# Reordering three edges of a long one-core kernel and parting the attention's queries and keys

## The chip, the cores and the metric

The kernel runs on one core of a Trainium2 chip. Time is device microseconds (us) from a run of the whole program, and a comparison uses the median of several runs. The engines are PE (TensorE), DVE (VectorE), ACT (ScalarE), POOL (GpSimd) and SP (SyncE, used here to issue transfers); each works through its own list of instructions in order, and they meet through semaphores.

## The reference

Two blocks follow each other for one sequence of 512 tokens and 1024 features, in fp32. The first has two layers: an RWKV-7 time mix with its MLP, then forgetting attention with its MLP. The second has an mLSTM branch, which also reads 256 context tokens, and a Fourier branch. Cut to the three things that the change touches:

```
# RWKV-7 time mix: the decay, and the output with its bonus
w_log = -softplus(-(w0 + tanh(xw @ w1) @ w2)) - 0.5
decay = exp(-exp(w_log))
y     = group_norm(wkv7_scan(r, decay, k, v, -kk, kk * a)) * ln_w + ln_b
bonus = sum_over_head(r * k * r_k) * v
out   = ((y + bonus) * g) @ wo
# forgetting attention: 16 heads of 64, F = cumsum(log_sigmoid(f_logit))
q, k  = rms_norm(q, q_gain), rms_norm(k, k_gain)
s     = q @ k.T / sqrt(64) + F[t] - F[s],   s <= t
o     = softmax(s) @ v
x     = x + (1 + gt1) * ((o * sigmoid(gate)) @ w_o)
# mLSTM branch: modulated inputs of the latents and of the context
h     = rmsnorm(x, g) * (1 + sc) + sh
hc    = rmsnorm(ctx, g) * (1 + scc) + shc
```

## The kernel before

Everything lies feature-major: a tile is 128 features by 512 tokens, so a matrix of 1024 features by 512 tokens is eight tiles. The context's tiles are 128 by 256. Weights are streamed as blocks of 128 x 2048 words, 1 MB each, in two buffers of `wraw`. SP issues a block's load once the block two before it has been split (`load_weights`, line 480). POOL splits each block into a high part `whi` that fp32r holds exactly (line 530) and the remainder `wlo` (line 534), in `split_weights`. PE then multiplies in three fp32r products, `whi`·high, `whi`·low and `wlo`·high (`block_of`, line 586; `block_by_tile`, line 618). The inputs of each product are parted in the same way: ACT rounds to the high part, DVE subtracts for the low part. In the names below `...h` and `...l` (`oh`, `ol`, `hh`, `hl`, `h2h`, `h2l`) are these parts.

The order of the work is written out by hand: each engine has a function per phase, and what an engine does next is what stands next in its text. Four places matter.

**Decay reads** (RWKV inputs, ACT). `high(n)` does n pieces of one input's mix, each a `keep` (line 1157) and a `round_mix` (line 1164). `hidden` reads a hidden tile of the gate from PSUM (line 1176) and rounds it (line 1181). Then eight reads of the decay products into `cum` (line 1176 as well, in `read_out`) free the PSUM banks that PE writes them into.

**Bonus additions** (end of the RWKV layer, POOL). In this stretch POOL first splits two weight blocks, that of `g2` and the first of `wo`, then adds the bonus to the normed output in eight tiles (line 1638). DVE gates each sum (line 1533), ACT rounds it (line 1504), DVE takes the low part (line 1538), and PE multiplies by `wo`. SP's queue holds in this order: a modulation block, two loads of weights (line 480), another modulation block (line 1457), the modulation row (line 1463, needed by ACT's Silu, line 1508), and six more blocks. DVE's line 1525 multiplies these blocks with the row; its results scale the residual additions (line 1550).

**Attention.** The eight pairs of heads have four query tiles each: 32 steps s, with s // 4 the pair i and s % 4 the query tile t. A step has two items n (its two heads). PE runs, for each step, `scores` (two 64-row products of `q_sb` with `kk_sb`, line 2590, then for each head the forget sums, line 2594, and the mask, line 2596), `turn` (transposes of the exponentials, line 2606) and, per pair, `values` (line 2616) and `spread_sums` (line 2625). DVE takes the maximum (line 2768); ACT takes the exponential (line 2693) and copies the turned ones (line 2702). PE issues the scores of a step ahead of the turns of the step before. DVE also normalises the next pair's queries and keys (`norm`, line 2760; gains from line 2576) and gates, weighs and parts the output (lines 2782, 2787, 2791), of which ACT rounds the high part (line 2708). The products of `scores` are fp32 products:

```
pe.matmul(ps[:, score_bank(2 * s + h), :w], q_sb[rr, i, P * t:P * t + P],
          kk_sb[rr, i, :w], start=True, stop=False)
```

**Start of the mLSTM.** DVE works out the latents' norm in a chain of small operations (lines 693, 3207, 3209), copies a column of it (line 3210), then scales and parts the first two context tiles (`h_run(0, 2)`: lines 3189 and 3195), with ACT's rounding between them (line 3120). PE's first product there (line 2988) waits for the low part `h2l`. ACT's root for the second norm (line 3123) stands in front of those roundings.

Of the kernel before, what the change touches and what calls it, by code (L numbers as in the profile page):

```python
# [16 lines left out]
F32 = mybir.dt.float32  # L17
# [364 lines left out]
def program(nc, A, out, plan, vat, cat):  # L382
    ctx = ExitStack()
    with ctx:
# [553 lines left out]
        with nc.Block() as block:  # L938
# [207 lines left out]
            def _(act):  # L1146
# [75 lines left out]
                hidden_half(1, ACT.Copy)  # L1222
                act.wait_ge(*hid_ready.at(2))
                for n in range(2):
                    high(3)
                    hidden(hidg[:, n], ACT.Sigmoid, sgh[:, n])
                high(2)

# [4 lines left out]
                for g in range(KT):  # L1233
                    read_out(cum[:, g], ACT.Sigmoid, V("w0", g))
                    if g == 3:
                        qk_read_out(act, 0, 7)
                    elif g == 6:
                        fold_read_out(act, 0, 7)
# [193 lines left out]
        with nc.Block() as block:  # L1432
# [183 lines left out]
            @block.gpsimd  # L1616
            def _(pool):
                def stepped(o):
                    o.then_inc(*inverse_step.inc())
                    pool.wait_ge(*inverse_step.at(inverse_step.made))  # L1620
                for hf in HALVES:
                    pool.wait_ge(*blk_in.at(16 * (hf + 1)))
                    for s in range(1, 31):
                        n = 31 - s
                        part = tmp[:, :s * n].rearrange("p (i j) -> p i j", j=n)
                        row = tt[:, s:s + 1, s + 1:].broadcast_to([P, s, n])
                        col = tt[:, 0:s, s:s + 1].broadcast_to([P, s, n])
                        stepped(pool.tensor_tensor(part, row, col, ALU.mult))
                        stepped(pool.tensor_tensor(tt[:, 0:s, s + 1:], tt[:, 0:s, s + 1:], part, ALU.add))
                    stepped(pool.memset(tt.rearrange("p s t -> p (s t)")[:, 0::33], 1.0))  # L1630
                    pool.tensor_copy(tn, tt.rearrange("p s t -> p t s")).then_inc(*inverted.inc())
                pool.wait_ge(*corrected_by.at(nth["ER", 3, 1][1]))
                pool.memset(yrows[:].bitcast(F32), 0.0).then_inc(*y_cleared.inc())
                split_weights(pool, firsts["wo"][1] + 1)
                for p in range(KT):
                    pool.wait_ge(*vb_shifted.at(p + 1))
                    pool.wait_ge(*by_dve.at(nth["SP", p][1]))
                    pool.tensor_tensor(r_sb[:, p], r_sb[:, p], arena[:, 25 + p], ALU.add).then_inc(*y_added.inc())
                project_pool(pool)
# [870 lines left out]
        pr, ptr = tiles("pr", 64, 4), [tiles(f"ptr{b}", 8 + 4 * b, 4) for b in range(4)]  # L2510
        oh, ol = tiles("oh", 48, KT, F32R), tiles("ol", 32, KT, F32R)
        sums = fixed("sums", [P, 4, 2, 4])
        top = fixed("top", [P, 4])
        NI, NS = 8 * KT, 4 * KT
        phase_start()
        with nc.Block() as block:
# [6 lines left out]
            rooted, inverted, root_high = signal("qk_rooted"), signal("qk_inverted"), signal("root_high")  # L2523
            gain_spread, pair_normed = signal("scale_spread"), signal("qk_normed")
            scored, topped, raised = signal("scores"), signal("max_ready"), signal("exp_done")
            turned, copied, totalled = signal("p_turned"), signal("p_copied"), signal("values_done")
# [8 lines left out]
            def score_bank(n):  # L2535
                return n % 4
# [16 lines left out]
            def _(pe):  # L2553
# [25 lines left out]
                def scores(s):  # L2579
                    i, t = s // 4, s % 4  # L2580
                    if t == 0:
                        pe.wait_ge(*pair_normed.at(2 * i + 2))
                    if s >= 2:
# [3 lines left out]
                    w = P * (t + 1)  # L2587
                    for h in range(2):
                        rr = slice(64 * h, 64 * h + 64)
                        pe.matmul(ps[:, score_bank(2 * s + h), :w], q_sb[rr, i, P * t:P * t + P], kk_sb[rr, i, :w], start=True,  # L2590
                                  stop=False)
                    for h in range(2):
# [73 lines left out]
            def _(act):  # L2666
# [29 lines left out]
                def copy(n):  # L2696
# [3 lines left out]
                    if t == 0 and i >= 2:  # L2700
# [3 lines left out]
                                   ACT.Copy).then_inc(*copied.inc())  # L2704

                def round_of(i):
                    act.wait_ge(*weighted.at(i + 1))
                    act.activation(oh[:, i], otile[:], ACT.Copy).then_inc(*rounded.inc())
# [21 lines left out]
                for k in range(KT):  # L2730
                    read_g(k)
                fold_read_out(act, 11, 4)
                exp(0)
                exp(1)
                for n in range(NI):
# [3 lines left out]
                    if n % 8 == 3 and n > 8:  # L2739
                        round_of(n // 8 - 1)  # L2740
                round_of(KT - 1)
                squares_of_x(act, x_squared, x_added, 5)
# [3 lines left out]
            def _(dve):  # L2746
# [10 lines left out]
                def norm(i, j):  # L2757
                    x, gain = ((q_sb, qgs[:, 0:1]), (kk_sb, V("kg", 0)))[j]
                    dve.wait_ge(*gain_spread.at(2 * i + j + 1))
                    dve.scalar_tensor_tensor(x[:, i], x[:, i], gain, ps[:, VALUES if j else SPREAD], ALU.mult,  # L2760
                                             ALU.mult).then_inc(*pair_normed.inc())

                def maximum(n):
# [41 lines left out]
                norm(0, 0)  # L2805
                norm(0, 1)
                maximum(0)
                maximum(1)
                for s in range(NS):
                    i, t = s // 4, s % 4  # L2810
                    if t == 0 and i:
                        sum_inverse_of(i - 1)
                    if t == 2 and i + 1 < KT:
                        norm(i + 1, 1)
                    if s + 1 < NS:
# [5 lines left out]
                    elif t == 1 and i + 1 < KT:  # L2821
                        norm(i + 1, 0)
                    if t == 2 and i:
                        part(i - 1)
# [53 lines left out]
        with nc.Block() as block:  # L2878
# [194 lines left out]
            def _(act):  # L3073
# [43 lines left out]
                def round_h(n):  # L3117
                    src, gain, norm, shift, k, part, width = h_of(n)
                    act.wait_ge(*scaled.at(n + 1))
                    act.activation(h2h[:, k, part], ps[:, 4 + n % 2, :width], ACT.Identity, bias=shift).then_inc(*rounded.inc())  # L3120
                root(act, rooted)
                act.wait_ge(*mean_made.at(2))
                act.activation(stat2[:, 1], ps[:, 7, 8:12], ACT.Sqrt, bias=C("epsn")).then_inc(*rooted2.inc())
                fold_read_out(act, 14, 2)
                for n in range(KT + 3):
                    round_h(n)
# [57 lines left out]
            def _(dve):  # L3184
# [13 lines left out]
                def h_run(lo, hi):  # L3198
# [4 lines left out]
                    part_h(hi - 1)  # L3203
                dve.memset(gacc[:], 0.0).then_inc(*VE.up(sem("dve")))
                inverse_root(dve, rooted, inverted)
# [3 lines left out]
                dve.tensor_tensor(ps[:, 7, 8:12], ps[:, 7, 8:12], stat[:, 1], ALU.mult).then_inc(*mean_made.inc())  # L3209
                dve.tensor_copy(stat2[:, 0], stat[:, 1]).then_inc(*VE.up(sem("dve")))  # L3210
                h_run(0, 2)
                dve.wait_ge(*rooted2.at(1))
                dve.reciprocal(ps[:, 7, 12:16], stat2[:, 1]).then_inc(*gain_made.inc())
                dve.wait_ge(*gain_made.at(1))
                dve.tensor_tensor(stat2[:, 2], ps[:, 7, 12:16], stat[:, 1], ALU.mult).then_inc(*inverted2.inc())
                h_run(2, KT)
                dve.wait_ge(*spread2.at(1))
                h_run(KT, 2 * KT)
                chain = sem("dve")
                dve.wait_ge(*VE.last())  # L3220
# [910 lines left out]
```

## Time and profile before

| | us |
|---|---|
| median of 3 runs | 2545.86 (2544.88 to 2550.26) |
| profiled execution | 2549.13 |
| its span, with a mean granted TensorE clock of 0.987 | 2547.3 |
| attention, first scores to last values | 1027.8 to 1131.9 of the span |

The profiled execution is 3.3 us above the median of the runs. The times in the rows further down count from the start of its span. In a timeline row come start, length, engine, line, operation, what is written and what is read, tile shapes, and the number of neighbouring instructions that the row joins; lengths of neighbouring instructions can overlap, since a pipeline takes the next before the last has ended. In brackets stands the idle time before and what ended it. PEld is PE loading weights; SPq and ACTq are issues of transfers.

### The profile page before, as it was taken

What the parts mean: (1) busy time and instruction counts of PE and PEld (TensorE: products, weight loads), DVE (VectorE), ACT (ScalarE), POOL (GpSimd) and SP (SyncE); (2) the same over time, 40 slices, a digit from 0 to 9 for tenths busy, and PEclk for the clock granted to TensorE, in tenths of its full rate; (3) what the DMA queues carried; (4) which work ended last, traced back from release to release, by engine and by line L of the source; (5) the groups of instructions that cost most, each with busy time, mean ns of one, the idle gap of its engine ahead of it and who ended that gap; (6) DMA issues with size and microseconds to landing.
All of it is one profiled execution on the core that took longest, in us unless ns stands there. A gap on an engine that the chain in (4) does not pass through costs nothing. (4 is left out here: it accounts for less than half of the span.)

```text
span 2547.3 us, 36273 instructions
## 1 busy us (share of the span) xinstructions
PE 2452.7 (96%) x14664; PEld 1925.6 (76%) x14664; DVE 1245.2 (49%) x1849; ACT 743.6 (29%) x1439; POOL 1536.1 (60%) x784
## 2 busy tenths in 40 slices
PE   5999988999999999999999999999999999999998
PEld 4777766788888777667888877888775478787886
DVE  7647257775562244454444437877485643121112
ACT  5744423331120212543311212333324431111210
POOL 6874717677777776016988873533262067754774
PEclk9999999999999999999999999999999999999999
DMA  7322436566652222104656522323334273311221
GB/s 276 108 83 80 121 97 264 211 243 231 231 215 93 99 90 99 40 18 142 228 206 229 214 100 95 117 116 116 151 138 147 102 303 126 114 66 67 83 99 66
DMA packets 90334, 358.28 MB, mean 141 GB/s; under 512 B 27337, under 2 KB 41289, under 8 KB 52946
## 3 DMA queue, kind: packets, MB, share of 16 engines
q1 hardware_dynamic: 65712, 229.79, 24.9%
q10 hardware_dynamic: 24482, 126.50, 13.1%
q8 instruction: 103, 1.69, 0.3%
q14 instruction: 37, 0.30, 0.0%
HBM read 317.18 MB, written 39.06 MB: 140 GB/s over the span
## 5 line engine op out<-in xcount | busy, mean ns | idle before, releaser
L530 POOL TENSOR_TENSOR whi<-wraw,con_sb 128x512 fp32r<-128x512 f32 (+1 forms) x305 | 622.0, 2059 | 826.8 <-PE ps L586 606.5
L534 POOL TENSOR_TENSOR wlo<-wraw,whi 128x512 fp32r<-128x512 f32 (+1 forms) x305 | 796.4, 2632 | 12.9
L586 PE MATMUL ps<-hh,whi 128*128 128x512 f32 x936 | 365.7, 391 | 0.0
L586 PE MATMUL ps<-hh,wlo 128*128 128x512 f32 x936 | 364.2, 389 | 0.0
L586 PE MATMUL ps<-hl,whi 128*128 128x512 f32 x936 | 364.2, 389 | 0.0
L586 PEld LDWEIGHTS ps<-hh,whi 128*128 128x128 f32 x936 | 175.7, 188 | 41.0 <-issue 4.3
L586 PEld LDWEIGHTS ps<-hh,wlo 128*128 128x128 f32 x936 | 175.7, 188 | 36.7
L586 PEld LDWEIGHTS ps<-hl,whi 128*128 128x128 f32 x936 | 175.7, 188 | 35.9
L586 PE MATMUL ps<-midh,whi 128*128 128x512 f32 x512 | 199.7, 390 | 0.0
L586 PE MATMUL ps<-midh,wlo 128*128 128x512 f32 x512 | 199.2, 389 | 0.0
L586 PE MATMUL ps<-midl,whi 128*128 128x512 f32 x512 | 199.2, 389 | 0.0
L2373 DVE TENSOR_TENSOR midl<-rsq,midh 128x512 fp32r<-128x512 f32 x64 | 110.6, 1729 | 153.8 <-ACT midh L2330 153.8
L586 PE MATMUL ps<-h2h,whi 128*128 128x512 f32 (+1 forms) x464 | 173.6, 374 | 0.8 <-ACT hb L3635 0.7
L586 PE MATMUL ps<-h2l,whi 128*128 128x512 f32 (+1 forms) x464 | 171.3, 369 | 0.0
L586 PE MATMUL ps<-h2h,wlo 128*128 128x512 f32 (+1 forms) x464 | 171.1, 369 | 0.0
L2216 DVE SCALAR_TENSOR_TENSOR cond_w<-cond_w,ps 128x1024 f32<-128x1024 f32 x136 | 159.9, 1211 | 0.0
L2324 ACT ACTIVATE relu<-ps 128x512 f32<-128x512 f32 x64 | 38.3, 599 | 381.4 <-PE ps L586 364.9
L2379 DVE SCALAR_TENSOR_TENSOR x<-ps,mod,x 128x512 f32<-128x512 f32 x64 | 48.0, 750 | 189.1 <-PE ps L586 189.1
L586 PEld LDWEIGHTS ps<-midh,whi 128*128 128x128 f32 x512 | 96.1, 188 | 20.9 <-issue 1.1
L586 PEld LDWEIGHTS ps<-midh,wlo 128*128 128x128 f32 x512 | 96.1, 188 | 20.1
L586 PEld LDWEIGHTS ps<-midl,whi 128*128 128x128 f32 x512 | 96.1, 188 | 19.7
L3240 DVE SCALAR_TENSOR_TENSOR ps<-xm,vec_sb,ps 128x441 f32<-128x441 f32 (+3 forms) x160 | 105.1, 657 | 5.2
(518 smaller groups left out, 4618.5 us busy)
## 6 DMA issues: line engine op xcount, KB each, us to landing
wraw<-wst SPq DMA_DIRECT2D x162, 1024.0 KB, 4.8
cond_w<-wcond ACTq DMA_DIRECT2D x68, 1024.0 KB, 4.8
first_w<-wcond SPq DMA_DIRECT2D x8, 1024.0 KB, 14.0
mod_w<-wcond SPq DMA_DIRECT2D x8, 1024.0 KB, 13.4
d_v<-key_and_query ACTq DMA_DIRECT2D x4, 1536.0 KB, 5.4
d_s<-ssb ACTq DMA_DIRECT2D x4, 1536.0 KB, 5.2
sld<-d_s SPq DMA_DIRECT2D x4, 1536.0 KB, 6.3
vld<-d_v SPq DMA_DIRECT2D x16, 384.0 KB, 3.5
```

What stands on the lines that cost most here:

```text
L530: o = pool.tensor_tensor(whi[:, s, c], wraw[:, f, c], C("zero").broadcast_to([P, width]), ALU.add)
L534: o = pool.tensor_tensor(wlo[:, s, c], wraw[:, f, c], whi[:, s, c].bitcast(F32), ALU.subtract)
L586: o = e.matmul(ps[:, b, :nt], w[:, k, mc], x[:, k0 + k, t0:t0 + nt], start=first and k == 0 and j == 0, stop=final and k == nk - 1 and j == 2)
L2216: o = dve.scalar_tensor_tensor(cond_w[n % 2][:, m], cond_w[n % 2][:, m], 1.0, row_at[r], ALU.mult, ALU.mult, accum_out=cond_to[layer][2 * ...
L2324: act.activation(relu[:, n % 4], ps[:, b], ACT.Relu).then_inc(*AC.up(acc_free[b]))
L2373: dve.tensor_tensor(midl[n // KT % 2][:, n % KT], rsq[:, n % 4], midh[n // KT % 2][:, n % KT].bitcast(F32), ALU.subtract).then_inc(*mid_lo ...
L2379: dve.scalar_tensor_tensor(x_sb[:, m], ps[:, b], mod[layer][:, 40 + m:41 + m], x_sb[:, m], ALU.mult, ALU.add).then_inc(*VE.up(acc_free[b]))
L3240: dve.scalar_tensor_tensor(dst, src, w(kh, kw), dst, ALU.mult, ALU.add).then_inc(*VE.up(chain))
```

## The change

**Decay reads.** The two `hidden` reads follow each other, and the three pieces that stood before the second and the two behind it move: one behind the pair, one each behind reads 0, 1, 3 and 5 of `cum`. The first three stay.

**Bonus additions.** The split of `wo`'s first block moves behind the first four additions.

**Attention.** Queries and keys of a pair are parted: ACT rounds each into the new tile `qk_high` (two pairs deep), DVE subtracts to get the low parts, which lie in `oh` (queries) and `ol` (keys) until the output is written there. `scores` makes six fp32r products of 64 rows per step, high·high, high·low and low·high for each of the two heads. For pair i+1 ACT rounds in the loop behind items 3 and 4 of pair i, and DVE subtracts in pair i's step t = 2, behind the maxima. The first scores of a pair wait for `qk_parted` instead of `qk_normed`. The key's `norm` moves from t = 2 to t = 1, `part` of the output from t = 2 to t = 3.

**Start of the mLSTM.** DVE scales two context tiles ahead of the norm's chain and parts them behind the mean, ACT rounds them ahead of the second root. The copy goes (a reciprocal in its place behind the context's tiles), and the clearing of `gacc` moves behind all tiles.

```diff
@@ -1223,6 +1223,6 @@
                 act.wait_ge(*hid_ready.at(2))
+                high(3)
                 for n in range(2):
-                    high(3)
                     hidden(hidg[:, n], ACT.Sigmoid, sgh[:, n])
-                high(2)
+                high(1)
 
@@ -1234,2 +1234,4 @@
                     read_out(cum[:, g], ACT.Sigmoid, V("w0", g))
+                    if g in (0, 1, 3, 5):
+                        high(1)
                     if g == 3:
@@ -1633,4 +1635,5 @@
                 pool.memset(yrows[:].bitcast(F32), 0.0).then_inc(*y_cleared.inc())
-                split_weights(pool, firsts["wo"][1] + 1)
                 for p in range(KT):
+                    if p % 4 == 0:
+                        split_weights(pool, firsts["wo"][1] + p // 4)
                     pool.wait_ge(*vb_shifted.at(p + 1))
@@ -2511,2 +2514,3 @@
         oh, ol = tiles("oh", 48, KT, F32R), tiles("ol", 32, KT, F32R)
+        qk_high = tiles("qk_high", 70, 4, F32R)
         sums = fixed("sums", [P, 4, 2, 4])
@@ -2524,2 +2528,3 @@
             gain_spread, pair_normed = signal("scale_spread"), signal("qk_normed")
+            qk_rounded, qk_parted = signal("qk_rounded"), signal("qk_parted")
             scored, topped, raised = signal("scores"), signal("max_ready"), signal("exp_done")
@@ -2581,3 +2586,3 @@
                     if t == 0:
-                        pe.wait_ge(*pair_normed.at(2 * i + 2))
+                        pe.wait_ge(*qk_parted.at(2 * i + 2))
                     if s >= 2:
@@ -2587,6 +2592,7 @@
                     w = P * (t + 1)
-                    for h in range(2):
-                        rr = slice(64 * h, 64 * h + 64)
-                        pe.matmul(ps[:, score_bank(2 * s + h), :w], q_sb[rr, i, P * t:P * t + P], kk_sb[rr, i, :w], start=True,
-                                  stop=False)
+                    high, at = qk_high[:, 2 * (i % 2):2 * (i % 2) + 2], slice(P * t, P * t + P)
+                    for n, (q, k) in enumerate(((high[:, 0], high[:, 1]), (high[:, 0], ol[:, i]), (oh[:, i], high[:, 1]))):
+                        for h in range(2):
+                            rr = slice(64 * h, 64 * h + 64)
+                            pe.matmul(ps[:, score_bank(2 * s + h), :w], q[rr, at], k[rr, :w], start=n == 0, stop=False)
                     for h in range(2):
@@ -2705,2 +2711,8 @@
 
+                def round_qk(i, j):
+                    act.wait_ge(*pair_normed.at(2 * i + j + 1))
+                    if i >= 2:
+                        act.wait_ge(*scored.at(8 * i - 8))
+                    act.activation(qk_high[:, 2 * (i % 2) + j], (q_sb, kk_sb)[j][:, i], ACT.Copy).then_inc(*qk_rounded.inc())
+
                 def round_of(i):
@@ -2731,2 +2743,5 @@
                     read_g(k)
+                    if k == 5:
+                        round_qk(0, 0)
+                        round_qk(0, 1)
                 fold_read_out(act, 11, 4)
@@ -2740,2 +2755,4 @@
                         round_of(n // 8 - 1)
+                    if n % 8 in (3, 4) and n // 8 + 1 < KT:
+                        round_qk(n // 8 + 1, n % 8 - 3)
                 round_of(KT - 1)
@@ -2762,2 +2779,7 @@
 
+                def low_qk(i, j):
+                    dve.wait_ge(*qk_rounded.at(2 * i + j + 1))
+                    dve.tensor_tensor((oh, ol)[j][:, i], (q_sb, kk_sb)[j][:, i], qk_high[:, 2 * (i % 2) + j].bitcast(F32),
+                                      ALU.subtract).then_inc(*qk_parted.inc())
+
                 def maximum(n):
@@ -2806,2 +2828,4 @@
                 norm(0, 1)
+                low_qk(0, 0)
+                low_qk(0, 1)
                 maximum(0)
@@ -2812,4 +2836,2 @@
                         sum_inverse_of(i - 1)
-                    if t == 2 and i + 1 < KT:
-                        norm(i + 1, 1)
                     if s + 1 < NS:
@@ -2822,3 +2844,7 @@
                         norm(i + 1, 0)
-                    if t == 2 and i:
+                        norm(i + 1, 1)
+                    elif t == 2 and i + 1 < KT:
+                        low_qk(i + 1, 0)
+                        low_qk(i + 1, 1)
+                    if t == 3 and i:
                         part(i - 1)
@@ -3121,2 +3147,4 @@
                 root(act, rooted)
+                round_h(0)
+                round_h(1)
                 act.wait_ge(*mean_made.at(2))
@@ -3124,3 +3152,3 @@
                 fold_read_out(act, 14, 2)
-                for n in range(KT + 3):
+                for n in range(2, KT + 3):
                     round_h(n)
@@ -3203,3 +3231,4 @@
                     part_h(hi - 1)
-                dve.memset(gacc[:], 0.0).then_inc(*VE.up(sem("dve")))
+                scale_h(0)
+                scale_h(1)
                 inverse_root(dve, rooted, inverted)
@@ -3209,4 +3238,4 @@
                 dve.tensor_tensor(ps[:, 7, 8:12], ps[:, 7, 8:12], stat[:, 1], ALU.mult).then_inc(*mean_made.inc())
-                dve.tensor_copy(stat2[:, 0], stat[:, 1]).then_inc(*VE.up(sem("dve")))
-                h_run(0, 2)
+                part_h(0)
+                part_h(1)
                 dve.wait_ge(*rooted2.at(1))
@@ -3216,4 +3245,6 @@
                 h_run(2, KT)
+                dve.reciprocal(stat2[:, 0], stat[:, 0]).then_inc(*VE.up(sem("dve")))
                 dve.wait_ge(*spread2.at(1))
                 h_run(KT, 2 * KT)
+                dve.memset(gacc[:], 0.0).then_inc(*VE.up(sem("dve")))
                 chain = sem("dve")
```

What the new text does to the order of each engine, at three places, follows; the names in brackets are semaphores, many of them reused from earlier phases.

ACT, in the attention, one transition between two pairs; before, `oh` is the rounding of the output, the `pr` rows are exponentials and the `ptr` rows copies:

```order
L2702 ACTIVATE ptr_8442<-ps 128x2x128 [waits x_in1]
L2693 ACTIVATE pr,sums<-ps,top 128x384 [waits x_in1,x_normed]
L2708 ACTIVATE oh<-otile 128x512 [waits first_in6]
L2702 ACTIVATE ptr_8441<-ps 128x3x128 [waits x_in1]
L2693 ACTIVATE pr,sums<-ps,top 128x512 [waits x_in1,x_normed]
L2702 ACTIVATE ptr_8442<-ps 128x3x128 [waits x_in1]
L2693 ACTIVATE pr,sums<-ps,top 128x512 [waits x_in1,x_normed]
L2702 ACTIVATE ptr_8441<-ps 128x4x128 [waits x_in1]
L2693 ACTIVATE pr,sums<-ps,top 128x128 [waits first_in0,x_in1,x_normed]
```

Changed:

```order
L2708 ACTIVATE ptr_8442<-ps 128x2x128 [waits x_in3]
L2699 ACTIVATE pr,sums<-ps,top 128x384 [waits x_in3,x_in1]
L2720 ACTIVATE oh<-otile 128x512 [waits y_added]
L2716 ACTIVATE qk_high<-q_sb 128x512 [waits x_in0,cond_row_in]
L2708 ACTIVATE ptr_8441<-ps 128x3x128 [waits x_in3]
L2699 ACTIVATE pr,sums<-ps,top 128x512 [waits x_in3,x_in1]
L2716 ACTIVATE qk_high<-kk_sb 128x512 [waits x_in0,cond_row_in]
L2708 ACTIVATE ptr_8442<-ps 128x3x128 [waits x_in3]
L2699 ACTIVATE pr,sums<-ps,top 128x512 [waits x_in3,x_in1]
L2708 ACTIVATE ptr_8441<-ps 128x4x128 [waits x_in3]
L2699 ACTIVATE pr,sums<-ps,top 128x128 [waits first_in2,x_in3,x_in1]
```

The two roundings into `qk_high` stand behind the third query tile's exponentials and between the copies of the same tile, ahead of the last exponential of the pair.

POOL, at the end of the RWKV layer, from the clearing of `y_rows` to the end of the phase (L530 and L534 are the halves of a split, arena_all the additions); before:

```order
L1633 MEMSET y_rows 128x512 [waits inverted]
L530 TENSOR_TENSOR whi<-wraw,con_sb 128x2048 [waits w_loaded0]
L534 TENSOR_TENSOR wlo<-wraw,whi 128x2048 [waits w_high]
L530 TENSOR_TENSOR whi<-wraw,con_sb 128x2048 [waits w_loaded1]
L534 TENSOR_TENSOR wlo<-wraw,whi 128x2048 [waits w_high]
L1638 TENSOR_TENSOR arena_all<-arena_all 128x512 [waits squares_paired,bonus_shifted] x8
```

Changed:

```order
L1635 MEMSET y_rows 128x512 [waits inverted]
L530 TENSOR_TENSOR whi<-wraw,con_sb 128x2048 [waits w_loaded0]
L534 TENSOR_TENSOR wlo<-wraw,whi 128x2048 [waits w_high]
L1641 TENSOR_TENSOR arena_all<-arena_all 128x512 [waits squares_paired,bonus_shifted] x4
L530 TENSOR_TENSOR whi<-wraw,con_sb 128x2048 [waits w_loaded1]
L534 TENSOR_TENSOR wlo<-wraw,whi 128x2048 [waits w_high]
L1641 TENSOR_TENSOR arena_all<-arena_all 128x512 [waits squares_paired,bonus_shifted] x4
```

The second pair of L530 and L534 now stands between the fourth and the fifth addition.

DVE, at the start of the mLSTM (ctx_sb rows scale a context tile, h2l rows take its low part); before:

```order
L3204 MEMSET gacc 128x768
L693 RECIPROCAL stat<-stat 128x4 [waits rooted]
L3207 SCALAR_TENSOR_TENSOR ps<-ps,stat 128x4 [waits inverted]
L3209 TENSOR_TENSOR ps<-ps,stat 128x4 [waits x_in2]
L3210 COPY stat<-stat 128x4
L3189 SCALAR_TENSOR_TENSOR ps<-ctx_sb,coef,ps 128x256 x2
L3195 SCALAR_TENSOR_TENSOR h2l<-ps,ada,h2h 128x256 [waits first_in1] x2
L3213 RECIPROCAL ps<-stat 128x4 [waits x_normed]
L3215 TENSOR_TENSOR stat<-ps,stat 128x4 [waits x_in3]
```

Changed:

```order
L3217 SCALAR_TENSOR_TENSOR ps<-ctx_sb,coef,ps 128x256 x2
L693 RECIPROCAL stat<-stat 128x4 [waits rooted]
L3236 SCALAR_TENSOR_TENSOR ps<-ps,stat 128x4 [waits inverted]
L3238 TENSOR_TENSOR ps<-ps,stat 128x4 [waits x_in2]
L3223 SCALAR_TENSOR_TENSOR h2l<-ps,ada,h2h 128x256 [waits first_in1] x2
L3242 RECIPROCAL ps<-stat 128x4 [waits x_normed]
L3244 TENSOR_TENSOR stat<-ps,stat 128x4 [waits x_in3]
```

The two scalings come first, the norm's small operations stand between them and the low parts, and the copy and the clearing of `gacc` are gone from here.

## Rows read from the trace of the kernel before

**Rows 1.** Page, part 1: busy us (share of the span) x instructions.

```profile
PE 2452.7 (96%) x14664; PEld 1925.6 (76%) x14664; DVE 1245.2 (49%) x1849; ACT 743.6 (29%) x1439; POOL 1536.1 (60%) x784
```

**Rows 2.** Waits of PE: engine, line, what it waited for: total, times, longest.

```profile
PE ps L2606 <- ACT pr L2693: 6.3, 10, 2.2
...
PE ps L2988 <- DVE h2l L3195: 4.2, 1, 4.2
...
PE ps L1659 <- DVE arena_all L2120: 3.6, 1, 3.6
...
PE ps L586 <- ACT cum L1176: 2.6, 1, 2.6
```

**Rows 3.** Timeline of PE, with its weight loads (PEld), in the attention: start, length.

```profile
1043.56 2.38 PE L2616 MATMUL ps<-ptr,vtok 128*64 128x512 f32 x16
...
1049.25 1.13 PE L2590 MATMUL ps<-kk_sb,q_sb 64*128 64x512 f32 x4
...
1049.25 0.30 PEld L2590 LDWEIGHTS ps<-kk_sb,q_sb 64*128 64x128 f32 x4 [0.17 <-issue]
...
1051.79 0.49 PE L2590 MATMUL ps<-kk_sb,q_sb 64*128 64x128 f32 x4
...
1055.89 2.38 PE L2616 MATMUL ps<-ptr,vtok 128*64 128x512 f32 x16
```

**Rows 4.** Timeline of ACT, same stretch (in brackets the idle time before, and its end).

```profile
1049.14 0.39 ACT L2702 ACTIVATE ptr<-ps 128x256 f32<-128x256 f32 x1 [4.22 <-PE ps L2606]
...
1050.80 0.65 ACT L2708 ACTIVATE oh<-otile 128x512 fp32r<-128x512 f32 x1
```

**Rows 5.** Timeline of DVE, same stretch.

```profile
1050.90 1.29 DVE L2768 TENSOR_REDUCE top<-ps 128x1 f32<-128x512 f32 x2 [0.45 <-PE ps L2596]
...
1052.11 0.68 DVE L2791 TENSOR_TENSOR ol<-otile,oh 128x512 fp32r<-128x512 f32 x1
```

**Rows 6.** Timeline of PE, RWKV inputs.

```profile
177.19 0.79 PE L586 MATMUL ps<-hidh,whi 128*128 128x512 f32 x1 [2.21 <-ACT arena_all L1176]
```

**Rows 7.** Windows: length, busy us of PE, PEld, DVE, ACT, POOL; clock; DMA share; GB/s.

```profile
117.00:120.00 3.00, 2.81 (x26) 1.92 (x26) 1.91 (x2) 2.57 (x6) 0.76 (x1) 1.00 0.35 52
...
177.50:180.00 2.50, 2.50 (x7) 1.92 (x7) 2.47 (x2) 1.48 (x3) 1.31 (x2) 0.50 0.13 16
...
1033.00:1036.00 3.00, 3.00 (x12) 2.15 (x13) 1.58 (x3) 1.01 (x5) 0.00 (x0) 0.63 0.33 105
...
1036.00:1039.00 3.00, 3.00 (x15) 1.78 (x14) 1.33 (x3) 1.78 (x6) 0.00 (x0) 0.80 0.00 0
```

**Rows 8.** Timelines of POOL, DVE and SP's queue around the bonus additions.

```profile
399.68 3.59 POOL L530 TENSOR_TENSOR whi<-wraw,con_sb 128x2048 fp32r<-128x2048 f32 x1
...
403.93 1.47 DVE L2114 SCALAR_TENSOR_TENSOR y_rows<-y_high,con_sb,ps 32x128 fp32r<-32x128 f32 x4
...
407.91 9.93 POOL L1638 TENSOR_TENSOR arena_all<-arena_all 128x512 f32<-128x512 f32 x8
...
407.98 0.33 SPq L480 DMA_DIRECT2D wraw<-wst  x1
...
408.82 0.43 SPq L1463 DMA_DIRECT2D mod_row<-crow  x1
...
409.27 0.70 DVE L1533 TENSOR_TENSOR ps<-ps,arena_all 128x512 f32<-128x512 f32 x1 [3.88 <-POOL arena_all L1638]
...
447.57 1.22 DVE L1525 SCALAR_TENSOR_TENSOR mod_w<-mod_w,ps 128x1024 f32<-128x1024 f32 x1 [2.81 <-DMA mod_w<-wcond]
```

**Rows 9.** Windows, the stretch behind them (same columns).

```profile
415.00:455.00 40.00, 40.00 (x189) 32.71 (x188) 34.48 (x60) 7.62 (x13) 28.56 (x10) 0.99 1.01 422
```

**Rows 10.** Timelines of POOL and DVE, start of the mLSTM.

```profile
1548.23 3.60 POOL L530 TENSOR_TENSOR whi<-wraw,con_sb 128x2048 fp32r<-128x2048 f32 x1 [9.78 <-POOLq L2179]
...
1549.84 2.02 DVE L3210 COPY stat<-stat 128x4 f32<-128x4 f32 x1
```

**Rows 11.** Timeline of ACT at the decay reads.

```profile
115.91 2.49 ACT L1176 ACTIVATE cum<-ps,vec_sb 128x512 f32<-128x512 f32 x4
```

## The prediction, made before the changed kernel ran

> **What bounds the kernel now.** I read the page's busy shares first: PE is busy 96% of the span, no other engine more than 60% [rows 1]. So a cut counts if it shortens PE's own work or one of its idle gaps, and a step put on another engine counts as soon as PE has to wait for it. Then I read PE's waits [rows 2]. The three edges show there with one long wait each: the context tiles (4.2 us, for h2l), the bonus additions (3.6 us, line 1659, for arena_all) and the decay reads (2.6 us, for cum). The attention shows with 6.3 us over ten waits for its exponentials. Then came the timelines of the edited stretches, to see what starts when, and the windows for the granted clock.
>
> **Attention: what PE saves.** A step is one query tile of one pair of heads. Its two fp32 products, four PE instructions in the trace, become six fp32r products. The old ones take 0.49 us at 128 keys and 1.13 at 512 [rows 3], so 0.28 and 0.21 per 128 keys. The four instructions are, as I read them, four passes for the two heads, which run side by side in the two halves of the rows; three passes, priced in proportion, take 0.16 per 128 keys. That saves 0.05, 0.11, 0.16 and 0.21 over a pair's four steps; 0.1 of it I give up for the first step, in which six weight loads have to pass. So 0.4 us per pair, for eight pairs **-3.4 us**, all that PE can win here.
>
> Weight loads could eat this. The four old ones end 0.30 us after the step's start, while the products run on to 1.13 [rows 3]: loads lie beside products. The Trainium skill, "TensorE: Matmul & The Clock Gate", section "The mechanism", says that a load overlaps a running product only where the row groups differ; by it each head's second and third product would show its load, an estimated 0.1 us each, some 7 us over 32 steps, and the parting would lose on PE itself. The row shows loads hidden in both halves, and the sum goes by the row.
>
> **Attention: what is put in front of PE.** Each pair needs two roundings on ACT (as the one of oh, 0.65 us [rows 4]; 0.55 to 0.6 where the next one overlaps) and two subtractions on DVE (as that of ol, 0.68 [rows 5]). Neither engine is full: ACT idles 4.22 us earlier in the pair [rows 4]. But the place decides. The roundings of pair i+1 stand in ACT's order behind the exponentials of pair i's third query tile, and the first scores of pair i+1 now wait for the last subtraction, where before they waited for normalised keys, ready long before. By the pair whose values start at 1055.89: the oh rounding starts at 1050.80 [rows 4] and is done near 1051.3; the query's rounding ends at 1051.8; a copy and a 512-wide exponential of the pair before, together about 1.0 us, bring it to 1052.8; the key's rounding ends at 1053.4; DVE's subtraction, with its release, at **1054.2**. Before, those scores start at 1051.79 [rows 3]. DVE is no hindrance: its two maxima end at 1052.2 [rows 5], and the query's subtraction fits before the key's. So PE stands 2.4 us longer in front of a pair's first scores. Queued behind them on PE are the last two turns of the pair before, the second scores and then that pair's values. The waits for exponentials that these turns have today [rows 2] go into the stall, some 0.4 us of the 6.3 per pair; the cheaper products give back 0.4; releases cost 0.1 to 0.2 on each of four new hops. I take +2.2 net per transition. Seven transitions: +15.4; the last pair has no successor and gives 0.4 back: **+15.0** for the stage, in the period of a pair from 12.3 us (1043.56 to 1055.89 [rows 3]) to 14.5. The first pair's parting lies beside PE's query-gate blocks, and I cost it at nothing; without that cover it would be two roundings and two subtractions, 2.4 us once.
>
> **Attention: the clock.** The stall with its ends makes an idle of near 3.0 us. After the idle of 2.21 that ends at 177.19 [rows 6], the granted clock is 0.50, the level of 1.2 GHz [rows 7]; after that of 2.6 for cum [rows 2], just before 117, it stays at 1.00, 2.4 GHz [rows 7]. In the attention's own start it is 0.63 over 1033 to 1036 and 0.80 over the next three [rows 7]: (0.37 + 0.20) x 3 = 1.7 us lost at most, about 1.4 with what waits hide. I expect it in half of the seven transitions: **+5**, with 0 and 7 x 1.7 = 12 as ends. Attention together **+20**, ends +15 and +27.
>
> **Bonus additions.** POOL now does four additions, then the split of wo's first block, then four. Before, the split starts at 399.68 and the additions behind it at 407.91, so it takes 8.2. The eight additions take 9.93, 1.24 each, and DVE's first gating waits 3.88 us for the first of them, to 409.27 [rows 8]; PE's 3.6 hangs on DVE behind that. With four additions first, at 399.7, the gating follows DVE's work of 403.93 + 1.47, so at 405.4, and PE's wait is gone but for a rest of 0.4: 3.2 earlier there, and by the time that wo begins I keep **-2.7**. The other queue pays. SP's load of wo's third block waits for the split of the first (issued at 407.98 [rows 8]); that now ends at 399.7 + 4.97 + 8.2 = 412.9. Behind it on SP stand the modulation blocks (one before the row, six after) and the modulation row (408.82 [rows 8]): all 4.95 later, and from 415 to 455 the transfers fill the DMA engines (share 1.01 [rows 9]), so nothing is made up. ACT needs the row before it rounds the last two tiles of wo's input. DVE's modulation products already wait 2.81 us for a block at 447.57 [rows 8], and the residuals stand behind them; so the end of this stretch, where DVE and PE end together, goes 4 to 5 later. I take **+4**, with -2.7 (the delay absorbed) and +5 as ends.
>
> **Context tiles first.** PE idles 4.2 for h2l [rows 2]. A copy of four columns at 1549.84 takes 2.02 us and ends with POOL's first split half (1548.23 + 3.60 [rows 10]); the context scalings stand behind it. Now they stand ahead of it and of the memset, and a reciprocal behind all tiles of the context replaces the copy. At the start -2.0 (the copy alone) to -2.8 (with the memset); afterwards DVE paces PE, so what is won stays. I take **-2.4**, ends -1 (POOL's weights late instead) and -3.5.
>
> **Decay reads.** PE idles 2.6 [rows 2], since ACT does high parts up to the reads at 115.91, four in 2.49 us [rows 11]. Now the reads come first, but the same number of high parts falls between and behind them, and PE's fold and the key projection wait for ACT's end of both. A third of the idle is my share: **-0.9**, ends 0 and -2.6.
>
> **Sum.** -0.9 + 4.0 - 2.4 + 20 = +20.7 against the profiled execution, 2549.13. That lies 3.3 above the median of the runs, 2545.86, on which I put it: **2566 us**. About 0.2%, 5.1 us, is what can be told from no change.
>
> **Rivals.** (a) *The clock stays at 2.4 GHz.* For it: 2.6 us idle did not lower it before 117 [rows 2, 7]. Sum +15.7: **2562**. (b) *The parting is hidden, and PE alone sets the pace.* It decides as soon as the last subtraction ends by 1052.2, within 0.4 us of today's start, that is with ACT's two roundings in the 4.22 us where it idles [rows 4] or 2 us earlier than I read them. Against it: they stand in ACT's order behind that idle. Then -3.4 - 0.9 - 2.4 and, with the SP delay absorbed, -2.7, in all -9.4: **2536**, faster; with the SP delay -2.7, 2543, no change to tell. (c) *The six products don't run side by side, or the clock falls longer.* Six passes one after another take 0.32 per 128 keys in place of 0.21, 8.8 us over the 80 key tiles instead of -3.4, or seven falls cost 2 to 3 us each: attention +32, **2578**. (d) *The SP delay is absorbed*, all else as forecast: -6.7, **2560**. (e) *The two late edges don't do what they say*, since another instruction of the same engine is late instead: 3.3 lost, **2570**.
>
> **How the numbers follow.** Forecast and (e) 0.48, (a) and (d) 0.22, (c) 0.12: all slower, 0.82. Rival (b) 0.12 faster; its version with the SP delay 0.06, no change. The range takes in the forecast, (a), (d), (e) and (c): from 2553 (a stall of 1.4 per transition, without falls of the clock, +9.6 - 0.4, and edges -2) to 2581 (attention +31, edges +4): **2553 to 2581**, leaving out 0.18 below it.
>
> **What would show it.** In the changed profile: PE idle by near 3 us before seven pairs' first scores, released by DVE's subtraction; a period of 14.5; granted clock under 1.00 behind some of them; a 512-key step shorter than 1.06; wo's third block issued near 413; h2l's wait down to 1.5 to 2; none of 2.6 for cum. I am wrong if a pair's period is 12.3 us or less, or a 512-key step takes longer than 1.06.

## The result and the profile after

The changed kernel takes 2585.59 us (median of 4 runs, 2582.89 to 2589.26) against 2548.06 before: a ratio of 1.0146, 95% interval 1.0134 to 1.0159, so **+37 us (34 to 40)**. The sign was forecast, the size was not: 2566 with a range to 2581. The profiled execution took 2589.26, its span 2587.5, with a granted clock of 0.977.

The busy shares (page, part 1, as [rows 1]) hardly move. PE is busy 20 us longer although its scores have a pass fewer, and idles longer too:

```profile
PE 2473.1 (96%) x14728; PEld 1941.6 (75%) x14728; DVE 1266.3 (49%) x1865; ACT 749.9 (29%) x1455; POOL 1536.3 (59%) x784
```

PE's waits, as in [rows 2] (total, times, longest):

```profile
PE ps L2597 <- DVE ol L2782: 17.8, 7, 2.6
PE ps L586 <- POOL wlo L534: 9.5, 2, 8.9
...
PE ps L2612 <- ACT pr L2699: 3.0, 3, 1.7
...
PE ps L3014 <- DVE h2l L3223: 1.6, 2, 0.9
...
PE ps L777 <- ACT qk_out L795: 1.5, 1, 1.5
...
PE ps L586 <- ACT cum L1176: 0.4, 1, 0.4
```

The first row is the forecast stall, seven times. The second is new and was not forecast. The other edges read as forecast: h2l from 4.2 to 1.6, cum from 2.6 to 0.4, with 1.5 for qk_out in its place.

**One transition between pairs.** PE, timeline (1057.04 and 1159.90 are the values of the first and the seventh pair; the rows with DVE in brackets are the first scores of pairs, each behind a stall):

```profile
1051.02 0.47 PE L2597 MATMUL ps<-qk_high 64*128 64x128 f32 x2 [2.16 <-DVE ol L2782]
...
1057.04 4.25 PE L2622 MATMUL ps<-ptr,vtok 128*64 128x512 f32 x16
...
1064.49 0.50 PE L2597 MATMUL ps<-qk_high 64*128 64x512 f32 x2
1064.83 0.40 PE L2597 MATMUL ps<-ol,qk_high 64*128 64x512 f32 x2
1065.06 0.40 PE L2597 MATMUL ps<-qk_high,oh 64*128 64x512 f32 x2
1065.39 0.49 PE L2600 MATMUL ps<-f_split,pick_r 128*128 128x512 f32 x1
...
1069.55 0.33 PE L2597 MATMUL ps<-qk_high 64*128 64x128 f32 x2 [2.60 <-DVE ol L2782]
...
1086.69 0.33 PE L2597 MATMUL ps<-qk_high 64*128 64x128 f32 x2 [2.60 <-DVE ol L2782]
...
1102.14 0.47 PE L2597 MATMUL ps<-qk_high 64*128 64x128 f32 x2 [2.60 <-DVE ol L2782]
...
1159.90 2.38 PE L2622 MATMUL ps<-ptr,vtok 128*64 128x512 f32 x16
```

The second and third pair of weight loads in the 512-key step begin while products still run:

```profile
1064.60 0.19 PEld L2597 LDWEIGHTS ps<-ol,qk_high 64*128 64x128 f32 x2
1064.83 0.19 PEld L2597 LDWEIGHTS ps<-qk_high,oh 64*128 64x128 f32 x2
```

A 512-key step takes 0.90 us from start to start (1064.49 to 1065.39), against 1.06 before (1049.25 to 1050.31 on the timeline of [rows 3]). The period of a pair is (1159.90 - 1057.04) / 6 = 17.1 us, against 12.3 [rows 3] and 14.5 forecast. The chain in front of the stall, ACT and then DVE, same stretch:

```profile
1066.04 0.65 ACT L2720 ACTIVATE oh<-otile 128x512 fp32r<-128x512 f32 x1
1066.56 0.64 ACT L2716 ACTIVATE qk_high<-q_sb 128x512 fp32r<-128x512 f32 x1
1067.08 0.50 ACT L2708 ACTIVATE ptr<-ps 128x384 f32<-128x384 f32 x1
1067.45 0.71 ACT L2699 ACTIVATE pr<-ps,top 128x512 f32<-128x512 f32 x1
...
1068.11 0.66 ACT L2716 ACTIVATE qk_high<-kk_sb 128x512 fp32r<-128x512 f32 x1
```

```profile
1068.80 0.69 DVE L2782 TENSOR_TENSOR ol<-kk_sb,qk_high 128x512 fp32r<-128x512 f32 x1 [0.87 <-ACT qk_high L2716]
```

From the oh rounding's start to the scores it is 1069.55 - 1066.04 = 3.5 us; the prediction had 1054.2 - 1050.8 = 3.4. The stall came as read. What it did to the clock did not. Windows, columns as [rows 7]:

```profile
1051.00:1061.00 10.00, 9.98 (x44) 6.60 (x46) 1.54 (x5) 3.44 (x14) 0.00 (x0) 0.51 0.00 0
1061.00:1069.00 8.00, 5.95 (x54) 4.49 (x50) 5.86 (x10) 4.62 (x14) 0.00 (x0) 1.00 0.01 2
1071.00:1078.00 7.00, 7.00 (x30) 3.88 (x30) 1.58 (x5) 3.13 (x12) 0.00 (x0) 0.51 0.00 1
1088.20:1091.60 3.40, 3.40 (x19) 2.51 (x19) 1.53 (x4) 2.00 (x8) 0.00 (x0) 0.50 0.00 0
```

With each of the seven stalls comes a stretch of 3 to 10 us at 1.2 GHz, and then, at 2.4 GHz, the next stall. PE is busy through nearly all of such a stretch (9.98 of 10.00 us in the first window): turns, second scores and the values, of which the first pair's are 4.25 us long in place of 2.38. What a fall takes goes with its length: from one pair's first scores to the next's it is 15.45 us with the shortest (1086.69 to 1102.14), 17.14 with one of about 7 us (1069.55 to 1086.69) and 18.53 with one of about 10 (1051.02 to 1069.55).

**The bonus additions.** POOL's split of the last block of wo, before and after, and what PE waits for then:

```profile
443.63 3.60 POOL L530 TENSOR_TENSOR whi<-wraw,con_sb 128x2048 fp32r<-128x2048 f32 x1 [3.09 <-DMA wraw<-wst]
```

```profile
451.85 3.60 POOL L530 TENSOR_TENSOR whi<-wraw,con_sb 128x2048 fp32r<-128x2048 f32 x1 [13.82 <-DMA wraw<-wst]
...
460.10 0.80 PE L586 MATMUL ps<-hh,whi 128*128 128x512 f32 x1 [8.92 <-POOL wlo L534]
```

SP issued that block's load earlier than before (427.44, before 429.88), but it landed 8 us later. SP's queue, after:

```profile
413.32 0.43 SPq L1459 DMA_DIRECT2D mod_w<-wcond  x1
413.80 0.43 SPq L1465 DMA_DIRECT2D mod_row<-crow  x1
414.67 4.55 SPq L1459 DMA_DIRECT2D mod_w<-wcond  x6
427.44 42.34 SPq L480 DMA_DIRECT2D wraw<-wst  x4
```

The modulation row goes out at 413.80, 4.98 later than in [rows 8], as forecast, and so do wo's third block and four modulation blocks around the row. The last three modulation blocks go out when they did before (417.92, before 417.86): they wait for the last addition, whose end has not moved. PE's wait of 3.6 us for arena_all [rows 2] falls to 0.4, and wo begins 2.45 us earlier; then 8.9 us are lost from 451 on.

### The profile page after: what moved, and what is told of

It is laid out like the page before. It is cut to its first block and busy times, and to the rows that moved or that the text cites. A ratio compares the mean times of both kernels' runs of the same rounds, so it can differ in the third digit from the quotient of the medians.

```text
span 2587.5 us, 36445 instructions
## 1 busy us (share of the span) xinstructions
PE 2473.1 (96%) x14728; PEld 1941.6 (75%) x14728; DVE 1266.3 (49%) x1865; ACT 749.9 (29%) x1455; POOL 1536.3 (59%) x784
## 5 line engine op out<-in xcount | busy, mean ns | idle before, releaser
L530 POOL TENSOR_TENSOR whi<-wraw,con_sb 128x512 fp32r<-128x512 f32 (+1 forms) x305 | 622.1, 2059 | 866.3 <-PE ps L586 603.6
L534 POOL TENSOR_TENSOR wlo<-wraw,whi 128x512 fp32r<-128x512 f32 (+1 forms) x305 | 796.4, 2631 | 12.8
```

What stands on the lines that cost most here:

```text
L530: o = pool.tensor_tensor(whi[:, s, c], wraw[:, f, c], C("zero").broadcast_to([P, width]), ALU.add)
L534: o = pool.tensor_tensor(wlo[:, s, c], wraw[:, f, c], whi[:, s, c].bitcast(F32), ALU.subtract)
```

## The experiments

All times are differences to the kernel before, run beside each; ratios with 95% intervals.

**Each part alone.** `only_attn`, `only_bonus`, `only_context` and `only_decay` are the kernel before with the hunks of one part of the diff and no other edit.

> The attention's part alone, the three edges as before. Theory A (read from the trace of the changed kernel): the attention alone costs some +33 us, seven stalls of about 2.6 us, each with a fall of the granted clock behind it. Theory B (the prediction's terms): +20 us, the rest of the 38 us comes from the edges or from parts working on each other. Between 30 and 36: A; 17 to 24: B.

Ratio 1.0124 (1.0109 to 1.0140): **+31.6 us (28 to 36)**. Theory A; the prediction's +20 falls. The trace has seven stalls, but a fall of the clock with six of them only:

```profile
1040.97 0.33 PE L2594 MATMUL ps<-qk_high 64*128 64x128 f32 x2 [2.17 <-DVE ol L2779]
...
1055.34 0.33 PE L2594 MATMUL ps<-qk_high 64*128 64x128 f32 x2 [2.60 <-DVE ol L2779]
...
1070.84 0.34 PE L2594 MATMUL ps<-qk_high 64*128 64x128 f32 x2 [2.60 <-DVE ol L2779]
...
1087.89 0.33 PE L2594 MATMUL ps<-qk_high 64*128 64x128 f32 x2 [2.60 <-DVE ol L2779]
```

```profile
1041.00:1055.00 14.00, 11.58 (x94) 8.36 (x94) 7.45 (x15) 8.14 (x28) 0.00 (x0) 1.00 0.01 1
1071.00:1077.80 6.80, 6.80 (x34) 5.19 (x36) 2.14 (x6) 3.08 (x14) 0.00 (x0) 0.50 0.00 1
```

Between the first two, with the clock at 1.00 throughout, it is 14.37 us from scores to scores; between the last two, with 1.2 GHz for about 7 us, 17.05. So one trace alone prices the fall apart from the stall, at 2.7.

> The order of the bonus additions alone. Theory A: +8 to +9 us, all in one wait of PE for the split of the last block of wo, whose load lands some 8 us later. Theory B (the prediction's term): +4 us, by the modulation blocks, and no such wait of PE.

Ratio 1.0023 (1.0014 to 1.0032): **+5.9 us (3.6 to 8.2)**. The time lies between the theories; the trace decides: PE's one long wait for the split is there.

```profile
PE ps L586 <- POOL wlo L534: 10.1, 2, 9.6
```

> The context tiles first, alone. Theory A: -3 us, the 4.2 us wait of PE for h2l falls to about 1. Rival: POOL's low part of the weights is late next, and the gain is under 1 us.

Ratio 0.9987 (0.9978 to 0.9996): **-3.3 us (-5.6 to -1.0)**; the wait for h2l falls from 4.2 to 1.1.

> The decay reads alone. Theory A: the 2.6 us wait for cum goes, but a wait for qk_out (1.5) and a later wait for a transfer take its place: between -0.5 and +0.5 us, nothing to tell. Theory B (the prediction's term): -0.9 us that stays to the end. The total can't tell them; the place where PE's lead is lost again can.

Ratio 0.9993 (0.9983 to 1.0003): -1.8 us, not to be told from nothing. PE waits 1.5 for qk_out as in the changed kernel. Where the lead is lost could not be told from one trace: PE's wait for the transfer of d_turn alone is 0.6 us here, 2.8 in the kernel before and 3.8 in the changed one.

The parts add up to +32.4; together they measure +37 (34 to 40). The difference is within the intervals of five measurements.

**The stall without the fall of the clock.** On top of `only_attn`, with these lines put behind the wait for earlier exponentials (`raised`):

```
+ if t == 0 and i:
+     for _ in range(11):
+         pe.matmul(ps[:, score_bank(2 * s)], unit_r[:, 0], f_split[:, 0], start=True, stop=True)
  pe.wait_ge(*qk_parted.at(2 * i + 2))      # first scores of pair i
```

> The attention's part alone, and in front of the first scores of pairs 1 to 7 PE makes eleven idle products of 512 columns (about 2.5 us) into a bank that the scores overwrite, then waits for the parted keys as before; what is computed stays. Theory A (the stall itself costs 2.2 us a transition, the fall of the granted clock behind it the rest): the clock stays at 1.00 in the attention and the loss falls from +32 to about +15 us. Theory B (the stall's hops, or the six products, are dearer than I priced them, the clock is a by-product): the loss stays above +25 us.

Ratio 1.0049 (1.0033 to 1.0064): **+12.5 us**. PE, timeline: the values of two pairs and the idle products between, and the window's clock:

```profile
1049.07 2.37 PE L2622 MATMUL ps<-ptr,vtok 128*64 128x512 f32 x16
...
1056.85 2.77 PE L2590 MATMUL ps<-f_split,unit_r 128*128 128x512 f32 x11
...
1063.45 2.37 PE L2622 MATMUL ps<-ptr,vtok 128*64 128x512 f32 x16
```

```profile
1055.00:1065.00 10.00, 9.76 (x65) 6.90 (x63) 5.48 (x12) 8.06 (x26) 0.00 (x0) 1.00 0.00 1
```

The period is 14.4 us, 2.04 more than before, almost the forecast 2.2, at a clock of 1.00. With PE idle instead it is 17.1 in the changed kernel. So the stall costs 2.0 a transition, as the 14.37 of the one transition without a fall in `only_attn` says too, and what idle does to the clock on average another 2.7: 31.6 - 12.5 = 19 us over seven, 14 to 25 by the two intervals (16 between the two traces). Theory B falls. PE did more work here and the kernel was faster for it.

**A shorter stall.** On top of `only_attn`, ACT's order behind item 3 of a pair:

```
- if n % 8 == 3 and n > 8:
-     round_of(n // 8 - 1)
- if n % 8 in (3, 4) and n // 8 + 1 < KT:
-     round_qk(n // 8 + 1, n % 8 - 3)
+ if n % 8 == 3 and n // 8 + 1 < KT:
+     round_qk(n // 8 + 1, 0)
+     round_qk(n // 8 + 1, 1)
+ if n % 8 == 4 and n > 8:
+     round_of(n // 8 - 1)
```

> The attention's part alone, with both roundings of the next pair directly behind the third tile's exponentials and the output's rounding one item later. The subtraction ends about 1.05 us sooner, so PE's stall is 1.5 to 1.6 us in place of 2.6. Stall itself: 7 x 1.1 = +8 us. If the granted clock falls behind each stall all the same (19 us by the difference of the two runs before): +25 to +28; if it falls behind none: +8 to +10. In between: the falls grow rarer with the shorter stall.

Ratio 1.0079 (1.0063 to 1.0094): **+20.2 us (16 to 24)**, in between. The stall is 1.58 each time; in the trace the clock falls behind four of the seven:

```profile
1054.07 0.33 PE L2594 MATMUL ps<-qk_high 64*128 64x128 f32 x2 [1.58 <-DVE ol L2780]
...
1084.56 0.33 PE L2594 MATMUL ps<-qk_high 64*128 64x128 f32 x2 [1.58 <-DVE ol L2780]
```

```profile
1054.00:1064.00 10.00, 9.93 (x66) 7.30 (x68) 3.06 (x9) 4.53 (x16) 0.00 (x0) 0.66 0.00 1
1084.00:1094.00 10.00, 9.28 (x80) 6.80 (x82) 5.13 (x12) 5.17 (x19) 0.00 (x0) 1.00 0.01 2
```

A pair behind which the clock stays has a period of 13.3, that is 12.3 and the 1.0 of the stall; one with a fall takes up to 15.5, from values to values. The traced execution, 2565.53 us, is the fastest of four (to 2574.1), so the others may have had more or longer falls. Why one stall of the same length is followed by a fall and the next is not, these runs do not show.

**Parting one pair earlier.** On top of `only_attn`: pairs 0 and 1 are normalised ahead of the loop, then, in pair i,

```
- PE, t == 1:   scale(i + 1, 0), scale(i + 1, 1)
+ PE, t == 1:   scale(i + 2, 0), scale(i + 2, 1)
- DVE, t == 1:  norm(i + 1, 0), norm(i + 1, 1);   t == 2: low_qk(i + 1, 0), low_qk(i + 1, 1)
+ DVE, t == 0, ahead of gate: low_qk(i + 1, 0), low_qk(i + 1, 1);   t == 1: norm(i + 2, 0), norm(i + 2, 1)
- ACT, behind items 3 and 4:  round_qk(i + 1, 0);  round_qk(i + 1, 1)
+ ACT, behind item 1:         round_qk(i + 1, 0);  round_qk(i + 1, 1)
- DVE, t == 3:  part(i - 1)
+ DVE, t == 2:  part(i - 1)
```

with the waits of `scale` and `values` moved by one pair.

> The attention's part alone, with the next pair's norm, rounding and subtraction made one pair earlier, so that ACT rounds where it idles (behind the second tile's exponentials) and DVE subtracts ahead of the gate. Theory A (only the place of the parting costs): no stall in front of a pair's first scores, clock 1.00, -2 to -4 us against the kernel before. Theory B (the added work on ACT and DVE costs wherever it stands): +3 us or more.

Ratio 0.9989 (0.9980 to 0.9998): **-2.8 us (-5.1 to -0.5)**. No stall is left in front of a pair's first scores, the period is 12.13, and the clock stays at 1.00 through the attention:

```profile
1046.94 2.37 PE L2619 MATMUL ps<-ptr,vtok 128*64 128x512 f32 x16
...
1059.07 2.37 PE L2619 MATMUL ps<-ptr,vtok 128*64 128x512 f32 x16
```

```profile
1033.00:1132.00 99.00, 92.80 (x734) 65.42 (x734) 60.89 (x121) 68.77 (x216) 0.00 (x0) 1.00 0.06 21
```

So the six products win most of what was forecast: from a step's first product to its first forget sum it is 0.48, 0.55, 0.72 and 0.89 us over a pair's four steps, before 0.42, 0.63, 0.85 and 1.06. That is 0.32 of the 0.4 per pair, of which the period shows 0.2. Another 2.1 us of the trace's gain come ahead of the first values (13.65 us from the first scores, before 15.75), where the clock of [rows 7], 0.63 and 0.80, is 1.00 here. The roundings and subtractions are all still there and cost nothing that shows: the 32 us hung on their place.

**The bonus additions and SP's queue.** `bonus_sp` is `only_bonus` with the load of wo's third block issued behind the second modulation block and the row; `sp_only` is the same move in the kernel before; `bonus_w3` is `only_bonus` with the load of the last block ahead of modulation blocks 5 to 7.

```
  load_cond(sp, 1)
  sp.dma_start(row[:], A["crow"][0])
+ load_weights(sp, ahead(*rwkv_inputs)[0] + 1)     # bonus_sp, sp_only: moved here from ahead of load_cond(sp, 1)
  ...
  sp.wait_ge(*y_added.at(KT))
+ load_weights(sp, firsts["wo"][1] + 4)            # bonus_w3 only
  for n in (5, 6, 7):
      load_cond(sp, n)
```

> The order of the bonus additions alone, and on SP the load of wo's third block moved behind the second modulation block and the modulation row (1.5 MB that no longer wait for POOL's split). Theory A (the loss is the transfers that begin 5 us later): most of it comes back, -3 to +2 us against the kernel before, and PE's wait for wo's last split falls from 9 to below 3. Theory B (POOL's later split is what counts): still +6.

Ratio 1.0013 (1.0004 to 1.0022): **+3.3 us (1.0 to 5.6)**. POOL waits 10.19 for wo's last block in place of 14.48 in `only_bonus`, PE 5.3 in place of 9.6. So less than half of the wait goes, not the two thirds that A asked for, and the two times, +5.9 and +3.3, have intervals that overlap: neither theory is met in full.

> The kernel before with SP's order of the run above and nothing else. Both theories: -1 to +0.5 us, since POOL waits only 3 us for one block there and PE for none. If it gains 3 us or more, the gain of the run above is not the additions'.

Ratio 1.0001 (0.9992 to 1.0010): +0.3 us (-2.0 to 2.6), nothing to tell, as expected.

> The order of the bonus additions alone, and on SP the load of wo's last block ahead of the modulation blocks 5 to 7 instead of behind them. Theory A (that load is late only because it queues behind blocks that all begin 5 us later): PE's wait of 9 us for the last split goes (below 2), but the three blocks land later and DVE waits for them instead; in time between +2 and +10 us. Theory B (POOL's own later start is what makes the split late): PE's wait stays above 6 us.

Ratio 1.0016 (1.0006 to 1.0027): **+4.1 us (1.5 to 6.9)**. POOL, then PE:

```profile
442.74 3.60 POOL L530 TENSOR_TENSOR whi<-wraw,con_sb 128x2048 fp32r<-128x2048 f32 x1 [2.67 <-PE ps L586]
```

```profile
458.15 0.47 PE L586 MATMUL ps<-hh,whi 128*128 128x512 f32 x1 [3.88 <-DVE x L1551]
```

The last block no longer waits for its load, so POOL's later start was not the cause; the place in the queue was. But now the modulation blocks land later, DVE's residuals with them, and PE waits 3.9 for a residual. Whichever goes first, something that PE needs comes late. That the stretch is too full of transfers to make up a start 5 us later is the prediction's reading [rows 9]; it fits both runs, but it wasn't tried with fewer bytes.

**The best of it.** `best` is `attn_ahead` with the decay reads and the context tiles of the change and the bonus additions as before; `joined` has the bonus additions of `bonus_sp` in place of the decay reads.

> Parting one pair earlier (as in the run attn_ahead), decay reads and context tiles as in the change, the bonus additions as before. If the parts add up: -2.8 - 1.8 - 3.3 = -8 us (-4 to -10), faster than the kernel before and than the changed one.

Ratio 0.9976 (0.9965 to 0.9986): **-6.1 us (-8.9 to -3.6)**, 2544.57 against 2551.46 beside it. It is faster than the kernel before, and 2585.59 of the changed kernel lies far above it.

> As the run best without the decay reads, but with the bonus additions' new order and SP's mended order (as in the run bonus_sp). If the parts add up: -2.8 - 3.3 + 3.3 = -3 us; some 5 us above the run best, so that the bonus order is not worth keeping.

Ratio 0.9982 (0.9973 to 0.9992): -4.6 us (-6.9 to -2.0). The 5 us that were to lie between the two runs measure 1.5, and the intervals overlap; the bonus order adds no gain and no loss that could be told.

## Why the prediction was wrong

- **The sign, and the attention's stall: right.** The chain in front of the first scores was read to 0.1 us (3.5 against 3.4), and the direct price to 0.2 (2.04 against 2.2, by the run with idle products). So was what PE saves: 0.16 in a step of 512 keys against 0.21, 0.32 in a pair against 0.4.
- **The clock: the term that was mis-sized.** The step that failed is "I expect it in half of the seven transitions: +5", with 12 as its end. The runs showed 19 (14 to 25): in the changed kernel's trace a fall comes with all seven, every transition is longer than 14.4, and a fall costs 2.7 on average, not 1.4. The 1.4 was taken from one fall at the attention's start [rows 7], which was a short one:

```profile
1033.80:1037.20 3.40, 3.40 (x12) 2.73 (x14) 2.47 (x4) 1.07 (x6) 0.00 (x0) 0.50 0.10 41
```

  A fall as short as that one costs 1.1 behind the stalls too (15.45 against 14.37), but five of the seven last about 7 or 10 us and cost 2.8 to 4.2. So the price for each us at 1.2 GHz, 0.3 to 0.4, was not too low in the prediction; the number of falls and their length were.
- **Rival (c)** had "seven falls cost 2 to 3 us each", which is what happened on average; it was given 0.12 and 2578. The parts measured one by one, +32.4 on the prediction's base of 2545.86, would also be 2578, inside the range. The changed kernel lies 4.6 above its end: 2.2 of that is the base (2548.06 beside the changed kernel), and the rest is less than the 5 us by which the whole exceeds its parts, which these intervals don't resolve.
- **Rival (a), for which the idle of 2.6 us before 117 spoke, fell.** One idle without a fall is no evidence that the next has none. In the trace of `only_attn`, whose decay reads are those of the kernel before, the same idle does have a fall behind it:

```profile
117.43 0.47 PE L586 MATMUL ps<-hidh,whi 128*128 128x512 f32 x1 [2.56 <-ACT cum L1176]
```

```profile
118.70:122.10 3.40, 3.40 (x23) 2.06 (x22) 0.91 (x2) 2.34 (x5) 0.00 (x0) 0.50 0.69 214
```

- **Bonus additions: the delay half right, its victim wrong.** The first part of SP's queue went 5 us later, as forecast; "all 4.95 later" did not hold for the last three modulation blocks, which are issued as before. The step that failed is "DVE's modulation products ... and the residuals stand behind them": it is wo's last block, issued behind the same queue, that came 8 us later, and PE stood 8.9 us for its split. Alone it is +5.9 against +4. That the size is near is in part luck: in the one trace of the whole change a wait of 8.9 that the prediction did not have stands against a start of wo 2.45 earlier, which it had (2.7).
- **Context tiles: right**, -3.3 against -2.4. **Decay reads:** -1.8 (-4.3 to 0.8) against -0.9, not resolved; the wait for qk_out came in place of that for cum, as said.
- **The rule on weight loads** (the Trainium skill, "TensorE: Matmul & The Clock Gate", section "The mechanism") did not hold here. With the prediction's estimate from it, 0.2 us a step, a 512-key step would have taken about 1.05; it takes 0.90, 0.05 more than the sum without the rule. The rows of weight loads above begin while products of the same row halves run, and the measurement decides.
- A slip in the working changes nothing: seven stalls of 1.4 are 9.8, not 9.6.

## What to carry to other kernels

Price a stall on PE twice: the time that it stands, and what the granted clock takes from the work behind it, and take the second from how long the clock stays low and what PE has to do in that stretch, not from one short fall in another place. Work that was added to idle engines was free here only when its position in their order lay ahead of its due time; moving it one iteration earlier turned +32 us into -3. When a queue is moved later, follow every transfer behind it to its consumer, the next phase's weights too, not only the one that already waits.

## What was not expected of the hardware

Eleven idle products in front of each pair's first scores made the kernel 19 us faster than leaving PE idle there: granted clock 1.00 in place of 0.50 behind the stall. The same idle of PE, 2.56 us for cum, has a fall of the clock behind it in one execution (`only_attn`) and none in another (the kernel before). And a load that is issued 2.4 us earlier (427.44 against 429.88) can land 8 us later, if the queue ahead of it was filled later.
